# Two-layer hybrid decoder trunk: the first quarter of the first expert selection done head by head

## The reference

```python
def peer_ffn(h, w_q, sub_keys, u_tab, v_tab):
    q = (h @ w_q).reshape(bsz, seq, PEER_HEADS, 2, PEER_HALF)      # 8 heads, 2 halves of 128
    s = jnp.einsum('blhpe,hpne->blhpn', q, sub_keys)               # 128 scores of each half
    s_top, i_top = lax.top_k(s, PEER_TOPK)                         # the best 16 of each
    cand = s_top[..., 0, :, None] + s_top[..., 1, None, :]         # 16 x 16 sums
    cand_idx = i_top[..., 0, :, None] * PEER_N_KEYS + i_top[..., 1, None, :]
    best, pos = lax.top_k(cand, PEER_TOPK)                         # 16 experts of each head
    idx = jnp.take_along_axis(cand_idx, pos, axis=-1)
    gate = jax.nn.softmax(best, axis=-1)
    # for each token and each of 8 x 16 experts e: gate * gelu(u[e] . h) * v[e]
    act = jnp.einsum('cd,ckd->ck', hc, u_tab[ic])
    return jnp.einsum('ck,ckd->cd', gc * jax.nn.gelu(act), v_tab[ic])
```

## Time and profile before

| | |
|---|---|
| median of three runs | 1794.7 us |
| the profiled execution | 1795.44 us, span 1793.6 us |
| TensorE busy | 1289.4 us (72%) |
| VectorE busy | 1126.5 us (63%) |
| ScalarE busy | 663.7 us (37%) |
| moved by DMA | 685.29 MB, mean 382 GB/s, of which gathers 536.90 MB |
| mean granted TensorE clock | 0.854 |

### The profile page before, as it was taken

One profiled execution on the slowest core, in us unless ns is written; L12 is line 12 of the kernel. 1 busy time (PEld: TensorE's weight loads), 2 busy tenths in 40 slices (PEclk: granted clock), 3 DMA queues, 4 the chain that ended last, 5 costly groups with the idle time before them and its releaser, 6 DMA issues.

```text
span 1793.6 us, 17530 instructions
## 1 busy us (share of the span) xinstructions
PE 1289.4 (72%) x5712; PEld 537.7 (30%) x5712; DVE 1126.5 (63%) x2528; ACT 663.7 (37%) x1983; POOL 623.6 (35%) x559
## 2 busy tenths in 40 slices
PE   3676545657876996897778789789987975545555
PEld 2364011112621333333336133353352620000000
DVE  8957989883558666435445766654453577676454
ACT  6524332222234328216423331751382243233222
POOL 5103334452232224324422322332332344444442
PEclk9897667889876998999989699899998986787676
DMA  7039899999997999999999899999999999999996
GB/s 313 1 123 397 337 423 413 409 407 419 422 423 304 409 423 419 425 423 421 422 423 423 337 367 425 421 367 420 423 378 411 422 349 421 410 417 413 420 422 282
DMA packets 88652, 685.29 MB, mean 382 GB/s; under 512 B 12144, under 2 KB 12272, under 8 KB 14320
## 3 DMA queue, kind: packets, MB, share of 16 engines
q0 software_dynamic: 73728, 536.90, 73.2%
q1 hardware_dynamic: 14832, 147.26, 19.7%
HBM read 683.08 MB, written 1.05 MB: 381 GB/s over the span
## 4 chain that ended last, share of the span: by engine, by line
DMA 35%; PE 33%; DVE 17%; ACT 6%; issue 5%; POOL 3%; SPq 1%; POOLq 0%; ACTq 0%; DVEq 0%
DMA ringmem<-experts,lay 24%; PE ps L437 11%; PE ps L407 10%; DMA wt<-w_qkv 7%; DVE ringmem L1068 6%; PE ps L447 4%; POOL ringmem L1039 3%; DMA wt<-w_o 2%; PE ps L422 2%; ACT lay L773 1%; DMA wt<-w_q 1%; ACT S L724 1%; PE ps L626 1%; PE ps L601 1%; PE ps L513 1%
## 5 line engine op out<-in xcount | busy, mean ns | idle before, releaser
L1039 POOL DMA_INDIRECT ringmem<-experts,lay x512 | 588.2, 1149 | 1084.4 <-PE ps L407 946.5
L407 PE MATMUL ps<-ringmem,S 128*32 128x512 f32 x2048 | 626.8, 774 | 393.8 <-ACT S L724 393.4
L1068 DVE CUSTOM_DVE_ANT_0 ringmem<-ringmem,Hrep 128x1024 f32<-128x1024 f32 x512 | 614.6, 1224 | 310.1 <-DMA ringmem<-experts,lay 300.6
L407 PEld LDWEIGHTS ps<-ringmem,S 128*32 128x32 f32 x2048 | 115.0, 128 | 817.4 <-ACT S L724 565.9
L719 ACT ACTIVATE gelus<-dots 128x2 f32<-128x2 f32 x256 | 51.6, 202 | 693.1 <-DVE dots L1068 692.2
L437 PE MATMUL ps<-wt,hT 128*128 128x512 f32 x576 | 256.2, 598 | 13.6 <-DMA wt<-w_qkv 13.5
L437 PEld LDWEIGHTS ps<-wt,hT 128*128 128x128 f32 x576 | 106.6, 190 | 163.3 <-issue 155.0
L715 ACT ACTIVATE S<-con,lay 128x32 f32<-128x32 f32 x512 | 134.3, 310 | 35.9 <-PE ps L407 35.8
L724 ACT ACTIVATE S<-S,gelus 128x32 f32<-128x32 f32 x512 | 136.9, 314 | 23.7
L447 PE MATMUL ps<-hT,wt 128*128 128x128 f32 x1024 | 119.8, 279 | 2.6 <-DMA wt<-w_q 1.5
L447 PEld LDWEIGHTS ps<-hT,wt 128*128 128x128 f32 x1024 | 117.1, 194 | 14.5 <-issue 6.3
(11 more groups left out here) (187 smaller groups left out, 1116.0 us busy)
## 6 DMA issues: line engine op xcount, KB each, us to landing
wt<-w_qkv SPq DMA_DIRECT2D x36, 2048.0 KB, 11.6
wt<-w_q SPq DMA_DIRECT2D x16, 2048.0 KB, 12.0
wt<-w_glu SPq DMA_DIRECT2D x5, 2048.0 KB, 12.5
ringmem<-experts,lay POOLq DMA_INDIRECT x512, 12.6
wt<-w_o SPq DMA_DIRECT2D x4, 2048.0 KB, 13.8
ringmem<-w_glu SPq DMA_DIRECT2D x3, 2048.0 KB, 17.1
gain<-gains SPq DMA_DIRECT2D x9, 512.0 KB, 15.0
area<-keys SPq DMA_DIRECT2D x4, 1024.0 KB, 9.6
```

The source lines that it names most:

```text
L407: last = pe.matmul(ps[TG * t:TG * (t + 1), half, :], S[:, u % 2, i, :], ring[:, (2 * u + i) % RING, D + half * 512:D + (half + 1) * 512], ...
L1039: pool.indirect_dma_start(ring[:, s % RING, :], None, experts[phase // NC], bass.IndirectOffsetOnAxis(ap=rows[:, phase % NC, j, n:n + 1], ...
L1068: last = v.tensor_tensor_reduce(ring[:, i, 0:D], ring[:, i, 0:D], Hrep[:, j, :], 1.0, 0.0, ALU.mult, ALU.add, dots[:, b, second:second + 1])
```

## The change

Quarter 0 of phase 0, and it alone, is done head by head. A head has 256 query columns, that is half of a projection, two of the four score matmuls, half of each top-k and 16 of the 32 steps.

- TensorE projects the first head's columns, scores them, spreads H, then projects the second head's columns (into another PSUM bank) and scores them, and then goes on as before with projections 1 to 3. The PSUM banks of the four quarters change in phase 0 (`BANKS0`).
- ScalarE copies the first head's q, the spread H, does the first head's gate; then copies the second head's q and the q of quarter 1, does the second head's gate, and copies the q of quarters 2 and 3.
- VectorE does the top-k of the first head, the scaling of tile 1's norm, the top-k of the second head, and then the pairs and the other quarters as before.
- GpSimd, ScalarE and VectorE may begin steps 0 to 15 when the first head's numbers are laid out. GpSimd and ScalarE wait for the second head's before step 16.
- SyncE issues the load of `gain` for tile 1's norm before the loads of weights 2 and 3, not behind them.

Since there is one event more, all counts that are waited for are shifted through a function `event`.

```diff
+        def event(ph, i, heads=(0, QH)):
+
+            if ph == 0 and i == 0:
+                return heads[1]
+            return QUARTERS * ph + i + 2
+
+        FIRST = [(0, 0, (h, h + 1)) for h in range(QH)]
+        BANKS0 = (5, 6, 7, 4)
...
             load_keys(0, glu_done, 1)
+            next_gain(2, 0)
             weights(0, 0, 6, 8)
-            next_gain(2, 0)
...
-            def project_turned(n, bank):
+            def project_turned(n, bank, parts=(0, 1, 2, 3), done=None):
...
-                    for m in range(4):
+                    for m in parts:
...
-                last.then_inc(w_used, 1)
+                last.then_inc(done or w_used, 1)
...
-                project_turned(item(0, 0, WQ0), 4)
+                project_turned(item(0, 0, WQ0), 4, parts=(0, 1), done=first_q)
                 pe.wait_ge(keys_in, 16)
-                score(0)
+                score(1, 4, 0, (0, 1))
                 spread_h(0, (0, 1, 2, 3))
+                project_turned(item(0, 0, WQ0), BANKS0[0], parts=(2, 3))
+                score(2, BANKS0[0], 0, (2, 3))
                 for i in range(1, QUARTERS + 1):
+                    if i == QUARTERS - 1:
+                        pe.wait_ge(best_ready, 1)
                     if i < QUARTERS:
-                        project_turned(item(0, 0, WQ0 + i), 4 + i)
+                        project_turned(item(0, 0, WQ0 + i), BANKS0[i])
                     if i >= 2:
-                        score(i - 1)
+                        score(i + 1, BANKS0[i - 1], i - 1)
...
-                copy_q(0)
+                copy_q(0, slice(0, 2))
                 act.wait_ge(z0_ready, KT)
                 spread_h(0, (0, 1, 2, 3))
-                gate_quarter(0, 0)
-                for i in range(1, QUARTERS):
-                    copy_q(i)
+                gate_quarter(*FIRST[0])
+                copy_q(0, slice(2, 4))
+                copy_q(1)
+                gate_quarter(*FIRST[1])
+                copy_q(2)
+                copy_q(3)
...
                 if at % QSTEPS == 0:
-                    pool.wait_ge(idx_ready, QUARTERS * phase + at // QSTEPS + 1)
+                    pool.wait_ge(idx_ready, event(phase, at // QSTEPS, (0, 1)))
+                if phase == 0 and at == QSTEPS // QH:
+                    pool.wait_ge(idx_ready, event(0, 0))
...
-                top_k(None, 0, 0, 0)
+                top_k(None, 0, *FIRST[0])
...
             norm_scale(1, norm_event(0, 1, 0), normed, h_spread, 2 * QUAD)
+            top_k(None, 0, *FIRST[1])
             other_quarters(0, 1)
```

More of the change, by code:

```diff
@@ L527, in first_scores, with score @@
                 pe.wait_ge(hT_ready, e + 1)
-                def score(i):
-                    pe.wait_ge(q_copied, i + 1)
-                    for m in range(QHP):
-                        last = pe.matmul(ps[:, 4 + i, m * P:(m + 1) * P], qT[:, i % 2, m, :],
+                def score(count, bank, i, parts=(0, 1, 2, 3)):
+                    pe.wait_ge(q_copied, count)
+                    for m in parts:
+                        last = pe.matmul(ps[:, bank, m * P:(m + 1) * P], qT[:, i % 2, m, :],
                                          keysT[:, QHP * i + m, :], start=True, stop=True,
@@ L554, in layer0 @@
                 else:
-                    pe.wait_ge(idx_ready, QUARTERS)
+                    pe.wait_ge(idx_ready, event(0, QUARTERS - 1))
                 s5_bu(c, 0)
@@ L1351, in find_experts @@
-                link(v.reciprocal(grec, gsum))
-                v.tensor_tensor(sel[:, 1, :].rearrange("p (h k) -> p h k", h=QH), gex,
-                                spread(grec, 2, [P, QH, TOPK]), ALU.mult).then_inc(sel_ready, 1)
+                link(v.tensor_reduce(found[:, :, steps], eq, AX.X, ALU.add))
+                if e > 1:
+                    v.wait_ge(idx_ready, e - 1)
+                v.scalar_tensor_tensor(out=sel[:, 0, steps], in0=found[:, 0, steps], scalar=float(NKEYS),
+                                       in1=found[:, 1, steps], op0=ALU.mult, op1=ALU.add)
```

149 lines of the change are left out of this document (85 added, 64 removed).

## The result

The changed kernel takes 1798.46 us (median of 20 runs) against 1793.62 us for the kernel before in the same session (20 runs). The ratio is 1.0032, with a 95% interval of 1.0023 to 1.0040: slower by 5.7 us, within 4.1 to 7.2 (the two medians by themselves are 4.8 us apart). One of its executions took 3813 us and is left out. The profiled execution took 1800.56 us, span 1798.8.

A forecast was written before the change was run, and what follows sets the result against it. VectorE bounds 160 to 220 us, then DMA; what delays VectorE's start delays everything. Projection 3's delay puts the first gelu at 165.0, pair 2 at 165.1 against 159.66: 1794.7 + 5.4 = 1800.1 us, range 1792.5 to 1803.

The forecast's parts named there:

- one mechanism: TensorE held by head 0's gate, VectorE's pair 2 by ScalarE's late gelu: +5.4 us; chance 0.50 at +3.5 or more.
- top-k of one head: VectorE's top-k for one head takes 8.7 us, against 15.5 for both, with 4.7 for maxima, replacements and indices.
- The early start: Head 0's numbers are ready at 128.2 instead of 140.07 us, so GpSimd starts gathers 11.9 us earlier.
- Half of projection 0: On TensorE, 3.5 us at the lower clock, then the higher; half the records done at about 114.6 us.
- The step that carried the sum: TensorE waits from 124.5 to 128.8 us for head 1's q, behind head 0's gate on ScalarE, delaying projections 1 to 3.
- the slack that the sum had subtracted: Between ScalarE's first gelu (154.61) and VectorE's pair 2 (159.66): 5.05 us of delay costs nothing.
- The second wait: Projection 3's weights take 11.6 us beside gathers; TensorE idles 3.3 us and projection 3 ends at 159.3.
- rival 1: Load as quick as before (7.8 us) or clock kept: +0.4 to +1.8 us; chance 0.32 including cases up to +3.5.
- The clock term: TensorE's clock falls in both waits; both at full clock give +1.8 us, one of two +3.5 or +3.7.
- Rival 2: Start of gathers decides, VectorE's wait for the first gather goes: 4.1 to 7.5 us faster; chance 0.12.
- Rival 3: As forecast, but ninth to twelfth gathers come 2 us late for pairs 4 and 5: +7 to +8 us; chance 0.06.
- The sign of being wrong: The constant shift from pair 2 to the last instruction: prediction wrong if pair 2's shift is missing at the end.

The follow-up runs named there:

- after: The first profiled execution of the changed kernel itself, compared with the kernel before: 1800.56 us; timed ratio 1.0032.
- e1: Changed kernel, with ScalarE copying head 1's q between head 0's exponential and its layout copies: ratio 1.0016 to the kernel before.
- e4: Kernel before, with one whole extra projection (7.3 us, result unused) on TensorE just ahead of projection 3: ratio 1.0021.
- e9: Changed kernel, with GpSimd holding gathers 3 to 8 until projection 3's weights have landed: ratio 1.0004 to the kernel before.
- e5: Changed kernel, with GpSimd holding gathers 5 to 8 until projection 3's weights have landed: ratio 1.0027 to the kernel before.
- e11: Changed kernel unedited, measured a second time on another chip: 1809.86 us against 1798.79 for the kernel before, ratio 1.0048.
- e7: Changed kernel, with head 1's q copied before head 0's layout and ScalarE's pairs 0 and 1 before the last q copy: 1794.42 against 1800.72 us, ratio 0.9969.
- e2: Changed kernel, with ScalarE doing its part of pairs 0 and 1 before copying quarter 3's q: ratio 1.0015 to the kernel before.
- e6: Kernel before, with only the gain load for tile 1's norm issued before the loads of weights 2 and 3: ratio 0.9991.
- e3: Changed kernel, with 16 extra unused matmuls on TensorE in its wait before head 1's scores: ratio 1.0046 to the kernel before.
- e8: As e7, with TensorE also doing pair 0's matmuls before projection 3: 1794.19 against 1800.72 us for the kernel before, ratio 0.9952.
- e12: The kernel of e8 timed once more on another chip: 1793.08 against 1798.79 us for the kernel before, ratio 0.9965.

## Why the prediction was right

The forecast, +5.4 us by one mechanism, met +5.7 [4.1, 7.2]. That it is so close is partly luck: the second measurement gave +8.6 [5.8, 11.5], and below two errors of the sum partly cancel. The mechanism is borne out step by step, with after's times less 2.1:

| step | predicted | measured |
|---|---|---|
| head 0's scores reach VectorE | 115.8 | 116.6 |
| top-k of one head | 8.7 | 9.3 |
| numbers of head 0 ready | 128.2 | 129.5 |
| TensorE waits for head 1's q | 4.3, clock falls | 4.42, clock fell |
| projection 1 ends | 138.7 | 139.3 |
| load of weights 3 | 11.6 | 11.75 |
| wait for it | 3.3, clock falls | 3.74, clock fell |
| projection 3 ends | 159.3 | 159.9 |
| from there to the end of the first gelu | 5.70 | 5.70 |
| VectorE waits for quarter 1's scores | 3.2 | 4.38 |
| VectorE waits for the gelu | 9.5 | 10.06 |
| pair 2 | +5.4 | +6.1 |

- **The early start was over-estimated.** The first gather comes 10.6 us earlier (8.5 in the trace, with the 2.1), not 11.9. Two terms were too small. Half of projection 0 takes 5.42 us and not 4.7. The 3.5 us at the low level were right; the records done in them were not. The 6 and 12 of the earlier trace rows count every record that touches a stretch of 1 us, so that many count twice; 64 records in 7.31 us are 8.8 a us at the full clock, half of that at the lower, and 3.5 + (32 - 3.5 x 4.4) / 8.8 is 5.4 us. The top-k of one head takes 9.3 and not 8.7: its maxima, replacements and indices take 5.3 us, more than half of 9.5. ScalarE's copy of head 1's q waits for both, so head 1's scores start 1.0 us later than predicted; those scores and projection 1 then take 0.4 less, and 0.6 to 0.7 us are left at pair 2, the difference between +5.4 and +6.1.
- **The step that carried the sum held.** TensorE, which had waited nowhere, waits in ScalarE's queue, and everything behind it is late; e1 takes 4.2 us off by that queue alone. e4 measured the slack that the sum had subtracted.
- **The second wait held for its reason.** The load is slow because gathers are outstanding: e9 shows it with 7.9 us and no gap. That also explains why rival 1 lost in this execution. The DMA stands idle behind it as the prediction said, between about 157 and 170: from 162 to 172 its share is at most 0.02 (160 to 170, less the 2.1).
- **The clock term was right in its place, and is not fixed.** In the profiled execution both gaps (4.42 and 3.74 us) cost the high level. In e5 and e11 a first gap of 2.83 to 2.84 us did not. The prediction had +3.5 or +3.7 for one of two gaps at the full clock; e5 came to +5.3 and e11 to +10.9. What the full clock gives back is there: in e5 head 1's scores start 1.2 us later than in after and projection 1's event comes 0.5 us earlier, 1.6 us in all (less the offsets). But in both traces the short gap comes of a low clock in projection 0, which had cost the 1.2 us and more beforehand, and in e11 the event of projection 1 came 3.5 us behind its last record. The prediction had neither term. Which share of the timed runs goes which way the times don't tell.
- **Rival 2** (faster) needed projection 3 to end by 149.9; in the changed kernel it ends at 159.9, so the condition was rightly seen not to hold. e7 gets there in another way: projection 3 ends at 156.2 (less the offset), but pair 2 no longer stands behind it. It is faster by 5.6 us by its ratio (interval 2.7 to 8.3), where rival 2 named 4.1 to 7.5.
- **Rival 3** did not happen: VectorE waits for no gather between 100 and 235 us. In e2, where pair 2 is early, it does.
- **The tail.** The shift of the gathered steps stays between 7.8 and 9.7 us (with the 2.1 in it) for most of the way up to 1660 us, with single steps from 5.7 to 10.0; it is 6.7 at the last step and 5.2 at the end, which less the 2.1 is 3.1 where the runs give 5.7. A drop over the last 140 us, of 0.8 to 3.3 us (2.8 in after), is in every kernel's trace against the one of before, so it belongs in part to that execution. The sign of being wrong that the prediction named, a shift not found again at the end, can't be judged from two traces: e6, which changes next to nothing, stands 0.4 us early at step 26, 10.3 late at step 200 and 3.6 late at the end. For the end only the timed runs count.

## What to carry to other kernels

When one engine's queue both hands out early results and serves another engine, starting earlier puts the hand-out in front of the service: place the few tenths of a microsecond that the other engine needs first (here one copy of 0.37 us ahead of 3.5 us of layout gave back 4.2 us). Work that starts a flood of DMA earlier also lengthens every load that now falls inside the flood, and it pays only if the consumers' waits behind that load are taken away too (e7 for ScalarE; that TensorE's pair 0 ahead of projection 3 adds to it is not shown). Measure the slack of the place that decides by putting in a known piece of work, as e4 did, before believing a subtraction. And before comparing two traces, compare them ahead of the first edit: here the clock there accounts for 1 to 3 us between executions.

## What the runs showed of the hardware that I had not expected

- **Gaps on a fully clocked TensorE while the gathers flow.** In e1, e2, e3, e7, e8, e11 and e12 the projections have gaps of 0.2 to 1.1 us labelled "issue" (1.1 to 2.0 us in sum, 0.8 in e12), the first of them 8 to 10.5 us after the first gather is issued. The changed kernel's first profiled execution and e9, whose TensorE was at the lower level after its gap, have none. Nor has e5, which kept its clock through a first gap of 2.84 us and had only four gathers outstanding: 128 records in one row of 14.46 us. In e2, e3 and e11 the end of projection 1 falls into such a stretch, and both engines that wait for it go on 2.7 to 3.6 us after its last record. Between 130 and 145 us one instruction packet of 0.02 MB moves, beside the gathers; this is the row of the DMA queues in that stretch for e11:

```profile
q8 instruction: 1, 0.02, 0.4%
```

  The Trainium skill, "Runtime: NRT & Kernel Launch", section "Instruction fetch mechanics", says that an engine's instructions come in blocks of 16 KiB over a DMA queue of its own; the packet's size agrees. That TensorE ran out of instructions because the block was slow beside the gathers would explain the gaps and the late event. The traces speak against it rather than for it: before, after and e9, which have no such gaps, show the same row; where there are gaps, the packet moves 3 to 8.5 us ahead of the first of them; and it takes about as long beside the gathers (6.2% of 16 engines in a stretch of 1 us, e11 at 136) as with nothing beside it (6.0%, before at 127). The cause of the gaps stays open.
- **A 2 MB load has two prices here**, 7.8 to 7.9 us with the gathers not yet begun or just through, 11.4 to 13.0 us beside four or more. Holding back four of eight took off no more than 0.4 us (e5, 11.4, against 11.75 in after and 12.0 in e11).
- **The clock behind a gap goes with what TensorE had before it, not with the gap alone.** First gaps of 2.83 us (e11) and 2.84 (e2, e5) left it at 1.00, those of 4.42 (after) and 4.43 (e9) did not. But the two groups are the two kinds of traces: the gap is 1.6 us shorter where the second half of projection 0 had just taken 5.3 to 5.4 us instead of 3.8 at a clock that had fallen before it. Which of the two matters, these traces don't separate. Ahead of projection 3, a gap of 1.97 us (e1) and one of 2.52 (e8) were enough to bring 0.50; before them TensorE had had its "issue" gaps.
